# Scan stage of a sequence-mixing block: rows split into f16 parts and turned by a DMA transpose, in place of f32 TensorE transposes

## What is computed

```python
y = ssd(xs, dt, a, bm, cm)                  # chunked scan, chunks of 128 tokens
y = y + d_skip[:, None] * xs
y = y.reshape(bsz, s, SSM_D_INNER) * jax.nn.silu(z_ssm)
y = rms_norm(y.reshape(bsz, s, SSM_GROUPS, SSM_D_INNER // SSM_GROUPS), ssm_norm_g)
y_ssm = y.reshape(bsz, s, SSM_D_INNER) @ w_branch_ssm
```

## Time and profile before

| | |
|---|---|
| three runs | 2745.0, 2740.7, 2744.49 us; median 2744.49 us |
| span of the profiled execution | 2738.7 us |
| TensorE busy | 2476.7 us (90% of the span) |
| VectorE busy | 1654.1 us (60%) |
| ScalarE busy | 1033.5 us (38%) |
| GpSimd busy | 629.3 us (23%) |
| mean granted TensorE clock | 0.959 of full speed |
| scan stages of groups 0 to 3 begin at | 1958.9, 2150.0, 2341.2, 2532.3 us |

### The profile page before, as it was taken

The page is one execution under the profiler, slowest core; times in us unless marked ns, Lnnn a source line. Parts: engine busy times, 40 slices in busy tenths (PEclk is TensorE's granted clock), DMA queues, the critical chain, the costliest instruction groups (busy, mean ns, idle before and its releaser), DMA issues. The chain is left out here.

```text
span 2738.7 us, 40825 instructions
## 1 busy us (share of the span) xinstructions
PE 2476.7 (90%) x15855; PEld 1326.7 (48%) x15855; DVE 1654.1 (60%) x2961; ACT 1033.5 (38%) x1594; POOL 629.3 (23%) x618
## 2 busy tenths in 40 slices
PE   4999985989799997699789989898999999999999
PEld 3556543545455554355334446644454444444444
DVE  6787774322233233576499988754774766757864
ACT  5111452221122222555544348822443533624620
POOL 2021020000000001331345410000540731712702
PEclk9999997999899999799899999999999999999999
DMA  8685575899999998220112210053002002011133
GB/s 245 205 290 177 197 268 196 316 386 391 389 386 370 385 350 300 84 70 16 39 39 85 95 52 2 17 208 131 8 1 100 8 1 100 9 52 49 66 116 126
DMA packets 131570, 433.12 MB, mean 158 GB/s; under 512 B 27792, under 2 KB 37392, under 8 KB 122960
## 3 DMA queue, kind: packets, MB, share of 16 engines
q1 hardware_dynamic: 95536, 349.13, 35.0%
q10 hardware_dynamic: 25696, 48.93, 5.0%
q0 software_dynamic: 10176, 32.78, 4.0%
HBM read 371.86 MB, written 58.94 MB: 157 GB/s over the span
## 5 line engine op out<-in xcount | busy, mean ns | idle before, releaser
L1484 PE MATMUL m_gu<-conv_y,m_xT 128*64 128x256 f32 x1024 | 233.6, 388 | 17.8 <-DMA arena<-in_moe_w_up 15.5
L2604 POOL TENSOR_TENSOR group_words<-group_words 128x1024 f16<-128x1024 f16 x64 | 149.8, 2361 | 373.7 <-PE i_pj L144 364.4
L1486 PE MATMUL m_gu<-arena,m_xT 128*64 128x256 f32 x1024 | 233.6, 388 | 0.0
L1563 DVE TENSOR_TENSOR m_hid<-m_sg,m_gu 64x256 f32<-64x256 f32 x96 | 39.6, 412 | 318.2 <-ACT m_sg L1532 318.2
L1486 PEld LDWEIGHTS m_gu<-arena,m_xT 128*64 128x64 f32 x1024 | 143.1, 140 | 73.9 <-issue 15.4
L1532 ACT ACT_TABLE_LOAD x48 | 61.6, 1283 | 305.8 <-issue 293.1
L1506 PE MATMUL m_y_ps<-arena,m_hidT 128*64 128x512 f32 x768 | 175.4, 598 | 0.0
L1484 PEld LDWEIGHTS m_gu<-conv_y,m_xT 128*64 128x64 f32 x1024 | 143.1, 140 | 36.0 <-issue 25.0
L142 PE MATMUL s_pj<-hT,arena 128*128 128x512 f16 x384 | 147.4, 384 | 12.7 <-issue 11.6
L142 PE MATMUL i_pj<-hT,group_words 128*128 128x512 f16 x384 | 146.5, 381 | 13.5 <-DVE group_words L357 8.0
L143 PE MATMUL s_pj<-hT,arena 128*128 128x512 f16 x384 | 147.1, 383 | 0.0
(11 more groups left out here) (594 smaller groups left out, 6634.7 us busy)
## 6 DMA issues: line engine op xcount, KB each, us to landing
arena<-in_moe_w_down SPq DMA_DIRECT2D x32, 2048.0 KB, 24.9
conv_y<-in_moe_w_gate SPq DMA_DIRECT2D x22, 2048.0 KB
arena<-in_moe_w_up SPq DMA_DIRECT2D x22, 2048.0 KB
hT<-in_moe_w_gate SPq DMA_DIRECT2D x10, 2048.0 KB
hT<-in_moe_w_up SPq DMA_DIRECT2D x10, 2048.0 KB
x_tok<-in_ada_w ACTq DMA_DIRECT2D x8, 2048.0 KB, 12.6
slot_out<-m_y ACTq DMA_DIRECT2D x96, 128.0 KB
arena<-in_w_gates SPq DMA_DIRECT2D x24, 512.0 KB, 4.2
```

The lines of the kernel that those rows point to most:

```text
L1484: g = nc.tensor.matmul(gu_ps[i][g_rows, 0:FFN // 2], lhsT=xT[:, c, :], rhs=k.wg[e % WEIGHT_SLOTS][:, c, cols], start=c == 0, stop=c == KC - 1)
L1486: u = nc.tensor.matmul(gu_ps[i][u_rows, 0:FFN // 2], lhsT=xT[:, c, :], rhs=k.wu[e % WEIGHT_SLOTS][:, c, cols], start=c == 0, stop=c == KC - 1)
L1563: nc.vector.tensor_tensor(hid[:, i, :], sg[:, i, :], gu_ps[i][u_rows, 0:FFN // 2], ALU.mult) \
L2604: return tuple(k.nc.gpsimd.tensor_tensor(k.y_U[:, t % 2, n], k.adt_parts[:, n, t, heads].unsqueeze(2).to_broadcast([P, HPG, P]), k.upto16. ...
```

## The change

A row is now split into its f16 parts before it is turned. `rows16(t)` is a view of chunk t of `x_ssm` (512 f32 per partition, no longer read by then) as two times 512 f16. DVE makes 1/rms and signals it (`rstd`); ACT writes the scaled row as f16 into the high half (a new activation with Copy and a scale); DVE writes the scaled row less the high part into the low half (one scalar_tensor_tensor). Both the scaling in place and the subtraction from `tr` are gone. Then SP issues one DMA transpose per chunk, `turn_rows`, from the 128x1024 f16 row (256 KB) into `yT`. TensorE's transposes, ACT's copy out of PSUM and the bank `tr` are gone. Jobs 0 and 8 of the branch wait for four such DMAs each. Between 1/rms and the low part, DVE now does the job of `end` (steps 6 to 9), which before stood at the head of the next step.

```diff
+        def turn_rows(sp, t):
+
+            sp.wait_ge(q["row_low"], t + 1)
+            sp.dma_start_transpose(yT.rearrange("p a c s -> p (a c) s")[:, :, t * P:(t + 1) * P],
+                                   rows16(t).rearrange("p a n -> p (a n)")).then_inc(turned_in[t // 4], 16)
...
                     sp.dma_start(k.mg_att[:, c], k.gates_dram[c]).then_inc(k.mg_att_in[c], 16)
+                for t in range(TT):
+                    turn_rows(sp, t)
+                for h in range(2):
+                    sp.wait_ge(turned_in[h], 16 * 4)
...
                 sp.dma_start(k.w_first[:, :, :], ins["w_xbc"][xbc_tiles(g + 1)[0]]).then_inc(next_in, 16)
+                for t in range(TT):
+                    turn_rows(sp, t)
                 sp.wait_ge(next_in, 16)
+                for h in range(2):
+                    sp.wait_ge(turned_in[h], 16 * 4)
...
-            def transposes(t):
-
-                pe.wait_ge(q["normed"], t + 1)
-                if t:
-                    pe.wait_ge(q["tr_low"], t)
-                for c in range(4):
-                    last = nc.tensor.transpose(tr[:, c * P:(c + 1) * P], k.z_ssm[:, t, c * P:(c + 1) * P],
-                                               k.const("ident"))
-                last.then_inc(q["tr_done"], 1)
-
             def branch(j):
                 m, a = jobs[j]
                 if j == 0:
                     pe.wait_ge(q["z_out"], TT - EARLY_Z)
                 if j == 0 or j == KC:
-                    pe.wait_ge(q["tr_high"], 4 + a // P)
-                    pe.wait_ge(q["tr_low"], 4 + a // P)
+                    pe.wait_ge(turned_in[a // HALF], 16 * 4)
                 if before(j) is not None:
                     pe.wait_ge(q["br_out"], before(j) + 1)
...
-                if t >= 2:
-                    transposes(t - 2)
...
                     nc.scalar.activation(ss[:, t - 1:t], ss[:, t - 1:t], ACT.Sqrt, bias=eps[:, :],
                                          scale=1.0 / GW).then_inc(q["std"], 1)
-                if t >= 2:
-                    act.wait_ge(q["tr_done"], t - 1)
-                    nc.scalar.copy(yT[:, 0, :, (t - 2) * P:(t - 1) * P],
-                                   tr[:, :].rearrange("p (c q) -> p c q", q=P)).then_inc(q["tr_high"], 1)
+                    act.wait_ge(q["rstd"], t)
+                    nc.scalar.activation(rows16(t - 1)[:, 0], k.z_ssm[:, t - 1, :], ACT.Copy,
+                                         scale=ss[:, t - 1:t]).then_inc(q["row_high"], 1)
...
-                if t - 1 in end:
-                    accumulate(dve, end[t - 1])
...
                     accumulate(dve, middle[t])
                 if 1 <= t <= TT:
                     dve.wait_ge(q["std"], t)
-                    step(v.reciprocal(ss[:, t - 1:t], ss[:, t - 1:t]))
-                    v.tensor_scalar(k.z_ssm[:, t - 1, :], k.z_ssm[:, t - 1, :], ss[:, t - 1:t], None, ALU.mult) \
-                        .then_inc(q["normed"], 1)
-                if t >= 2:
-                    dve.wait_ge(q["tr_high"], t - 1)
-                    h = yT[:, 0, :, (t - 2) * P:(t - 1) * P]
-                    v.tensor_tensor(yT[:, 1, :, (t - 2) * P:(t - 1) * P],
-                                    tr[:, :].rearrange("p (c q) -> p c q", q=P), h, ALU.subtract) \
-                        .then_inc(q["tr_low"], 1)
-            accumulate(dve, end[TT + 1])
+                    v.reciprocal(ss[:, t - 1:t], ss[:, t - 1:t]).then_inc(q["rstd"], 1)
+                if t in end:
+                    accumulate(dve, end[t])
+                if 1 <= t <= TT:
+                    dve.wait_ge(q["row_high"], t)
+                    v.scalar_tensor_tensor(rows16(t - 1)[:, 1], in0=k.z_ssm[:, t - 1, :], scalar=ss[:, t - 1:t],
+                                           in1=rows16(t - 1)[:, 0], op0=ALU.mult, op1=ALU.subtract) \
+                        .then_inc(q["row_low"], 1)
```

More of the change, by code:

```diff
@@ L2844, in ssm_scan_stage @@
         yd_ps, yo_ps, st_ps = (k.ps(f"y{g}_{n}", [P, GW], ctx=ctx) for n in ("yd_ps", "yo_ps", "st_ps"))
-        tr, br = k.ps(f"y{g}_tr", [P, HALF], ctx=ctx), k.ps(f"y{g}_br", [P, HALF], ctx=ctx)
+        br = k.ps(f"y{g}_br", [P, HALF], ctx=ctx)
+        rows16 = lambda t: k.x_ssm[:, t, :].bitcast(F16).rearrange("p (a n) -> p a n", a=2)
+        turned_in = [k.sem(f"y{g}_turned_in{i}") for i in range(2)]
         names = ("pool_in", "U_done", "seg_done", "cb_done", "E_done", "cbm_done", "M_done", "yd_done",
-                 "yo_done", "st_done", "state_done", "yo_read", "y_done", "gated", "squared", "std", "normed",
-                 "tr_done", "tr_high", "tr_low", "br_done", "br_out", "dve_step", "xd_done", "f_high", "f_low",
+                 "yo_done", "st_done", "state_done", "yo_read", "y_done", "gated", "squared", "std", "rstd",
+                 "row_high", "row_low", "br_done", "br_out", "dve_step", "xd_done", "f_high", "f_low",
                  "small", "z_done", "z_out")
```

## The result

| | kernel before | changed kernel |
|---|---|---|
| median of the runs | 2742.99 us (4 runs) | 2762.68 us (4 runs) |
| range | 2740.7 to 2745.0 | 2760.85 to 2770.97 |
| ratio of the changed kernel to the one before | | 1.0078, 95% interval 1.0066 to 1.0090 |

What follows compares the result with a forecast made beforehand. The prediction took DVE's 10.09 us per chunk to bound steps 2 to 5 of the scan, TensorE from step 7; +2.3 us in groups 0 to 2 and +16.0 in group 3 took 2744.5 to 2762.5 us, range 2747 to 2803.

Steps and rivals of the forecast that it cites:

- Group 3's queue: Group 3's scan: first four transposes land behind the gate loads, so job 0 starts 14.9 us later; +16.0 us in sum.
- The wait at job 1: Group 3, job 1: its 0.7 us wait for the eviction of job 0 goes, since DVE has caught up.
- The wait of 2.1 us at job 8: Job 8 of each group: TensorE idles 2.1 us for chunk 7's transpose, landing 5.6 us against a cover of 3.5.
- Groups 0 to 2: Scan stages of the first three groups: −1.35 for transposes, +2.1 at job 8, net +0.75 us each, +2.3 in all.
- price of a transpose: DMA queue: 5.6 us from issue to landing, ends 2.1 and 8.8; 2.1 us each in a full queue.
- job 8's cover of 3.5: Between chunk 7's low part and job 8 being due: 3.5 us, signals included, in which a landing costs nothing.
- The row for such a loss: TensorE's clock after a long idle stretch: 3.3 us at a granted 0.53, about 1.6 us, counted in group 3.
- DVE's cadence: Scan steps, L3070 to L3070, 10.09 us per chunk: 1.5 added against 1.47 removed, no change; bounds −0.3 and +0.5.
- The way to ACT: DVE's wait per chunk for ACT's high part: 0.57 us for ACT plus some 0.1 for two signals.
- TensorE's transposes: Scan stages: 16 us of busy time, mostly covered; only chunks 5, 6 and 7 count, 1.35 us per group.
- the risen cadence: Rival, every chunk on DVE: the way to ACT lies open, +10 us on the forecast, 2773 us; chance 0.08.
- The fast transposes: Rival, DMA queue: landing 2.1 to 3.5 us, 0.7 each in the queue, sum +4.3, 2749 us; chance 0.16.

Runs made afterwards that it cites:

- turns_before_gates: Changed kernel, but in group 3 SP issues the transposes of chunks 0 to 3 ahead of the eight gate loads: ratio to the kernel before 1.0058, median 2756.7 us.
- early_reciprocal: Changed kernel, but DVE makes 1/rms of the chunk before ahead of L3091 in place of behind L3096: ratio 1.0086 (1.0067 to 1.0105).

## Why the prediction was right

The time was forecast as 2762.5 us and came out as 2762.68. The direction and the main place were right. That the two times agree so closely is luck: the forecast of the four stages was +18 and they measured +22.2, the medians differ by 19.7, the median before is now 1.5 us below the one that the forecast started from, and terms erred against each other within the groups too.

- **Group 3's queue**, the main term: +16.0 forecast, +13.7 measured, and turns_before_gates confirms the mechanism. Job 0 was forecast 14.9 us later and is 13.9 later against the stage's start (77.6 us after it in place of 63.7). Two sizes in it were wrong and cancel in part. The loads were taken to end at 2602.5 in the kernel before, where the DMA share drops; but the last one, issued at 2594.05, landed 10.4 us later, at 2604.5, 72.1 us into the stage, and in the changed kernel it lands 72.8 us into it. The four transposes behind them take 4.7 us in place of 8.4. The wait at job 1 was given back as forecast. The clock was 0.50 until past 2632, so that job 0 took 5.2 us where it took 2.7 before, which is 2.5 us lost and not 1.6. The wait of 2.1 us at job 8 did not come. In sum 13.9 − 0.8 − 0.4 − 1.35 + 2.5 = 13.85 us, against 13.7 measured.
- **Groups 0 to 2**: +0.75 forecast each, +2.6, +2.6 and +3.4 measured, and for other reasons. One term that was mis-sized is the *price of a transpose*, 5.6 us to landing: it took 3.0. That lies inside the bounds, near the lower row of 256 KB, and inside job 8's cover of 3.5, so the 2.1 us term is zero.
- **The step that was left out** is what the waits add up to at job 1. The prediction said that the 1.31 us from job 0 would only move to job 1's wait, and that chunk 4's transposes were worth nothing because that wait swallows them. It priced this at nothing and did not look at the length. By its own terms the wait would have been 0.7 + 1.3 + 0.5 = 2.5 us. It became 4.0, because TensorE reaches job 1 by 1.0 us earlier against the stage's start and DVE's eviction comes 2.3 us later; and behind it the clock falls. That costs 1.6 us in group 0, and more in group 2. The row for such a loss was there and was used for group 3 alone.
- **DVE's cadence**: no change forecast, with bounds of −0.3 and +0.5; measured +0.27. The way to ACT was right in size (0.79 us of waiting, 0.67 forecast for ACT's part). The new instruction was taken at 0.85 us from start to start and takes 1.38, L3070 became 0.6 longer, and L3082 1.0 shorter. The 2.3 us by which the eviction, and with it job 1, comes later are 0.85 in the step before the steady ones, 0.87 in the four after it, and 0.6 from the longer L3070 just ahead of the eviction. That lies inside the forecast's bounds for a group, at their upper end. 2.3 + 1.6 − 1.35 = 2.6 us, which is the measured loss of groups 0 and 1.
- **TensorE's transposes**: 1.35 us per group forecast as all that counts, and 1.35 measured: from the end of job 1 to the end of the first group's stage it takes 40.35 us in place of 41.70. Issuing them twice gave 1.3. The reason given for the cover was not quite right, though. The prediction has TensorE waiting in effect for POOL at 2018.33 and going at DVE's 10.09 us in steps 2 to 5. In the kernel before, TensorE's outputs start 9.65 us apart without any wait between them:

```profile
1997.43 1.15 PE L2990 MATMUL y_yd_ps<-group_words 128*64 128x64 f32 x32
...
2007.08 1.15 PE L2990 MATMUL y_yd_ps<-group_words 128*64 128x64 f32 x32
```

  TensorE and POOL only happened to be ready at the same time there. DVE fell behind TensorE by 0.44 us per chunk, and the 1.31 us at job 0 are as much as three such chunks.
- Of the rivals, the risen cadence came true by its place but not by its mechanism: ACT's root was in time (over by 2018.31, L3102 starts at 2020.05), and early_reciprocal shows that removing the wait for ACT gives nothing. The fast transposes came true by price (3.0 us to landing, 1.2 us each behind one another against its 0.7), but its time of 2749 did not: groups 0 to 2 lack 12.6 us of it, by DVE's delay and the clock at job 1, and group 3 lacks 5.4, mostly by the queue.
- Of the signs that the prediction named, the wait of job 0 in group 3, its absence in groups 0 to 2 and the order on SP came. The wait at job 8 and an L3107 of 0.7 to 0.9 us did not: it took 1.46.

## What to carry to other kernels

Busy time of TensorE is not time saved: of 16 us of transposes 5 lay on the path, 1.35 us per group. The freed PSUM bank was worth more (3.4 to 4.5 us per group), once a job was moved into it, though most of that only undid the longer wait that the change had brought; against the kernel before, the groups gained 0.9 to 1.1 us. A step moved to a DMA queue is also moved behind all that stands in that queue; look at each program place separately, since the same code made TensorE wait 14 us for the queue in one group and not at all in three. And where waits are moved onto one another, add them up and ask whether the sum takes the clock down.

## What was not expected of the hardware

- A 128x1024 f16 DMA transpose out of and into SBUF: 1.23 us of SP's time to issue, 3.0 us to landing in an empty queue, about 1.2 us each behind one another (four after the last gate load). Behind eight loads of 512 KB, its issue took up to 4.9 us and its landing up to 9.7.
- DVE and POOL slow each other in SBUF so evenly that three orders of DVE's work had the same cadence to 0.06 us, while the single instructions ranged from 0.83 to 1.83 (L3082) and from 1.41 to 2.38 us (the low part, 0.74 when POOL is done), and POOL's pair of multiplies (L2604) took 4.19, 4.64 or 5.17 us. The duration of one DVE instruction there says little of what removing it is worth. The low part with one f16 input in place of two took 1.06 against 1.46 us, and the cadence fell by the same 0.4.
- Instructions that read PSUM as one input (L3091, 0.67 to 0.69 us) kept their time throughout.
